# Wide matmuls in the up-projection: a high weight block times high and low activations at once, the halves summed on VectorE

## The reference

```
h = rmsnorm(x, ffn_norm_g[l])
up = causal_dwconv(h @ w_ffn_up[l], ffn_dw_w[l], ffn_dw_b[l])
gt, val = jnp.split(up, 2, axis=-1)
x = x + (jax.nn.silu(gt) * val) @ w_ffn_down[l]
```

## Time and profile before

| | |
|---|---|
| median of 3 runs | 926.17 us (925.93 to 927.03) |
| profiled execution | 928.54 us, its span 926.7 us |
| busy share of the span | PE 93%, DVE 68%, ACT 52%, POOL 44% |
| mean granted clock | 0.973 |
| instructions | 18327, of them 6732 matmuls |
| matmuls of `uh`, `ul` with the unit weights | 3 x 832, mean 283 to 285 ns |

### The profile page before, as it was taken

How to read it: one execution, slowest core, us unless ns; L and a number is a source line. 1 busy time by engine, 2 the same in 40 slices (tenths; PEclk the granted TensorE clock), 3 DMA queues, 4 the chain that set the end, 5 groups by cost and what they waited for, 6 DMA issues and landing times.

```text
span 926.7 us, 18327 instructions
## 1 busy us (share of the span) xinstructions
PE 864.2 (93%) x6732; PEld 827.4 (89%) x6732; DVE 628.1 (68%) x1198; ACT 486.0 (52%) x730; POOL 405.8 (44%) x94
## 2 busy tenths in 40 slices
PE   2799999799999999999979999997999999999996
PEld 1799988678999999999979998785999999999995
DVE  6586899925367876656537878994445687666564
ACT  4353357636456555645555333873635655455454
POOL 4477735445721131131257874543565031321323
PEclk8799999989999999999989999997999999999998
DMA  7355424313535555555425542432434546555551
GB/s 259 112 181 183 163 92 137 137 47 136 181 137 182 182 181 181 181 184 180 179 95 182 183 182 92 138 137 66 162 116 158 182 143 217 182 184 181 181 181 46
DMA packets 20512, 144.20 MB, mean 156 GB/s; under 512 B 2400, under 2 KB 2656, under 8 KB 3296
## 3 DMA queue, kind: packets, MB, share of 16 engines
q1 hardware_dynamic: 19872, 142.62, 43.3%
q10 hardware_dynamic: 576, 0.75, 0.2%
HBM read 142.31 MB, written 1.05 MB: 155 GB/s over the span
## 4 chain that ended last, share of the span: by engine, by line
PE 67%; DVE 16%; issue 10%; ACT 5%; DMA 1%; DVEq 0%; ACTq 0%
PE pu L720 18%; PE pu L721 17%; PE pu L722 17%; DVE pc L493 5%; ACT whi L225 2%; PE ps L720 2%; PE ps L722 2%; PE ps L721 2%; DVE wlo L622 1%; DVE ol L557 1%; DVE top L534 1%; PE pc L722 1%; PE pt L721 1%; PE pt L720 1%; PE pt L722 1%
## 5 line engine op out<-in xcount | busy, mean ns | idle before, releaser
L197 POOL TENSOR_TENSOR wlo<-raw,whi 128x2048 fp32r<-128x2048 f32 x88 | 405.1, 4606 | 512.6 <-ACT whi L225 512.6
L225 ACT ACTIVATE whi<-raw 128x2048 fp32r<-128x2048 f32 x134 | 254.7, 1902 | 29.1 <-PE pu L722 26.2
L720 PE MATMUL pu<-hh,whi 128*128 128x256 f32 x800 | 233.1, 291 | 24.4 <-ACT hh L242 22.6
L720 PE MATMUL pu<-uh,whi 128*128 128x256 f32 x832 | 237.2, 285 | 5.4 <-DVE ul L600 3.2
L721 PE MATMUL pu<-ul,whi 128*128 128x256 f32 x832 | 235.4, 283 | 0.0
L722 PE MATMUL pu<-uh,wlo 128*128 128x256 f32 x832 | 235.4, 283 | 0.0
L721 PE MATMUL pu<-hl,whi 128*128 128x256 f32 x800 | 228.1, 285 | 0.0
L722 PE MATMUL pu<-hh,wlo 128*128 128x256 f32 x800 | 228.0, 285 | 0.0
L493 DVE SCALAR_TENSOR_TENSOR pc<-upad,par,pc 128x256 f32<-128x256 f32 x464 | 186.9, 482 | 0.3
L720 PEld LDWEIGHTS pu<-hh,whi 128*128 128x128 f32 x800 | 155.1, 194 | 28.4 <-ACT hh L242 23.3
L720 PEld LDWEIGHTS pu<-uh,whi 128*128 128x128 f32 x832 | 159.6, 192 | 7.8 <-issue 7.5
(11 more groups left out here) (142 smaller groups left out, 1170.5 us busy)
## 6 DMA issues: line engine op xcount, KB each, us to landing
raw<-in_weights SPq DMA_DIRECT2D x134, 1024.0 KB, 4.8
x<-in_x_t SPq DMA_DIRECT2D x2, 512.0 KB, 5.6
out_y<-qk SPq DMA_DIRECT2D x2, 512.0 KB, 2.6
par_all<-in_params ACTq DMA_DIRECT2D x1, 472.0 KB, 10.3
const<-in_const ACTq DMA_DIRECT2D x1, 130.0 KB, 7.1
probs<-in_positions ACTq DMA_DIRECT2D x1, 128.0 KB, 4.8
gf<-in_final_g ACTq DMA_DIRECT2D x1, 4.0 KB, 12.4
```

The lines of the kernel that those rows point to most:

```text
L197: nc.gpsimd.tensor_tensor(wlo[s][:, :], raw[s][:, :], whi[s][:, :].bitcast(f32), ALU.subtract).then_inc(lo_ready[s], 1)
L225: A(whi[s][:, :], raw[s][:, :], ACT.Copy).then_inc(hi_ready[s], 1)
L720: MM(out, whi[s][:, w], hi, start=start, stop=False, skip_group_check=accumulate)
```

## The change

The normalised activations of the up-projection are kept side by side in one tile `uparts` (for each input block 256 high, then 256 low columns). For an up unit each high weight block is multiplied by both at once, in one matmul of 512 columns that fills a PSUM bank: columns 0 to 255 collect the high sums, 256 to 511 the sums of high weight x low activation. The low weight block x high activation stays a matmul of 256 columns that adds to the first half. A unit so has 32 matmuls in place of 48 and needs two banks, one for the gate, one for the value half. The two pairs of banks take the place of `pu[0..2]` and `po`: the second pair's last bank is `po`, so the layer's second up unit now waits for the norm factor (`rstd_ready`) too.

Since VectorE is to sum two halves of one bank, ScalarE first copies the low halves into SBUF (`take_low`, into `low_sums`, which lies in `gate`), VectorE adds them to the high halves in place in PSUM, and then scales as before. Banks in other parts of the program keep their use under new names. The diff, cut:

```diff
+                def take_low(k, ab, s, done_value):
+
+                    act.wait_ge(unit_done[s], done_value)
+                    A(low_sums[:, ab, :, :], pairs[ab][:, :, 1, :], ACT.Copy).then_inc(low_taken, 1)
+
...
+                    take_low(k, 0, 2, l * USES + j + 12)
                     hidden_tile(k, 0, col, col + FT * 4, k - 1, lambda: split_high(l, 2, j + 11))
                     act.wait_ge(unit_done[1], l * USES + j + 12)
                     hidden_high(k, 0, parity)
+                    take_low(k + 1, 1, 0, l * USES + j + 13)
                     hidden_tile(k + 1, 1, col + 4, col + FT * 4 + 4, k, None if last else lambda: split_high(l, 0, j + 12))
...
-                def scale_up(s, ab, done_value):
-
-                    dve.wait_ge(unit_done[s], done_value)
-                    V.tensor_tensor(up[:, ab, :, :], pu[s][:, :, :], rstd[:, :].unsqueeze(1).to_broadcast([P, 2, T]),
+                def scale_up(k, ab):
+
+                    dve.wait_ge(low_taken, k + 1)
+                    sums = pairs[ab][:, :, 0, :]
+                    V.tensor_tensor(sums, sums, low_sums[:, ab, :, :], ALU.add).then_inc(up_whole, 1)
+                    dve.wait_ge(up_whole, k + 1)
+                    V.tensor_tensor(up[:, ab, :, :], sums, rstd[:, :].unsqueeze(1).to_broadcast([P, 2, T]),
                                     ALU.mult).then_inc(up_ready, 1)
...
+                            w = slice((2 * k + m) * P, (2 * k + m) * P + P)
+                            MM(pair[:, m, :, :], whi[s][:, w], uparts[:, k, :, :], start=(k == 0), stop=False)
+                            last = MM(pair[:, m, 0, :], wlo[s][:, w], uh[:, k, :], start=False, stop=(k == NT - 1))
+                    last.then_inc(unit_done[s], 1)
...
                 pe.wait_ge(down_zero, l + 1)
-                standard(U_FFN + 1, uh, ul)
+                pe.wait_ge(x_ready, l * 8 + 4)
+                pe.wait_ge(rstd_ready, l * 3 + 3)
+                up_unit((U_FFN + 1) % RING, uses(l, U_FFN + 1), pairs[1])
```

More of the change, by code:

```diff
@@ L81, in hybrid_encoder @@
         oh, ol = sb("oh", [P, NT, T], f32r), sb("ol", [P, NT, T], f32r)
[L82 removed]
+        uparts = sb("uparts", [P, NT, 2, T], f32r)
+        uh, ul = uparts[:, :, 0, :], uparts[:, :, 1, :]
         fh, fl = oh[:, 0:4, :], ol[:, 0:4, :]
@@ L113, in hybrid_encoder @@
         up = gate[:, 0, 0:4, :].rearrange("p (a n) t -> p a n t", a=2)
+        low_sums = gate[:, 0, 4:8, :].rearrange("p (a n) t -> p a n t", a=2)
         pos_i, turns = probs[0][:, 0:2, :].bitcast(i32), probsT[0][:, 2:4, :]
         ang, aabs = sb("ang", [P, 2, P])[:, :, :], sb("aabs", [P, 2, P])[:, :, :]
-        pu = [pb(f"pu{s}") for s in range(RING)]
+        pairs = [ctx.enter_context(nc.psum_tensor(f"pair{i}", [P, 2, 2, T], f32)) for i in range(2)]
+        pu = [pairs[0][:, 0, :, :], pairs[0][:, 1, :, :], pairs[1][:, 0, :, :]]
+        po = pairs[1][:, 1, :, :]
         ps = [pb(f"ps{i}") for i in range(2)]
-        pt, po, pc = pb("pt"), pb("po"), pb("pc")
+        pt, pc = pb("pt"), pb("pc")
         down = [ps[0], ps[1], pt, pc]
@@ L141, in hybrid_encoder @@
         gate_ready, m_step = sem("gate_ready"), sem("m_step")
-        down_zero, down_done, up_ready, f_conv0, f_tap, f_silu, f_ready, fh_ready, fl_ready = [
-            sem(n) for n in ("down_zero", "down_done", "up_ready", "f_conv0", "f_tap", "f_silu", "f_ready", "fh_ready", "fl_ready")]
+        down_zero, down_done, low_taken, up_whole, up_ready, f_conv0, f_tap, f_silu, f_ready, fh_ready, fl_ready = [
+            sem(n) for n in ("down_zero", "down_done", "low_taken", "up_whole", "up_ready", "f_conv0", "f_tap", "f_silu", "f_ready", "fh_ready", "fl_ready")]
         y_ready, y_out_s = sem("y_ready"), sem("y_out")
@@ L462, in _ @@
                 V.tensor_scalar(par[:, PA_CW:PA_CW + NT * CONV_WIDTH], par[:, PA_CW:PA_CW + NT * CONV_WIDTH], 0.5, None, ALU.mult).then_inc(par_ready, 1)
-                for pairs in (top, less_top):
+                for both in (top, less_top):
                     for g in range(N_KV):
                         sinks = par[:, PA_SINK + GROUP_PAIRS * g:PA_SINK + GROUP_PAIRS * (g + 1)]
-                        V.tensor_copy(pairs[:, N_CHUNKS * g:N_CHUNKS * (g + 1), :, 1],
+                        V.tensor_copy(both[:, N_CHUNKS * g:N_CHUNKS * (g + 1), :, 1],
                                       sinks.unsqueeze(1).to_broadcast([P, N_CHUNKS, GROUP_PAIRS])).then_inc(par_ready, 1)
@@ L866, in _, with up_unit @@
                 scaled = parts_ready(uh_ready, l * 8 + 4, ul_ready, l * 8 + 4)
-                standard(U_FFN, uh, ul, scaled, lambda: sum_pair(po[:, 0, :], sq, 3, sq_ready, l * 12 + 12))
+                def up_unit(s, uses_before, pair, ready=None, between=None):
+                    pe.wait_ge(hi_ready[s], uses_before + 1)
+                    pe.wait_ge(lo_ready[s], uses_before + 1)
+                    for m in range(2):
+                        if m == 1 and between is not None:
+                            between()
+                        for k in range(NT):
+                            if ready is not None and m == 0 and k % 2 == 0:
+                                ready(k // 2)
+                            w = slice((2 * k + m) * P, (2 * k + m) * P + P)
+                            MM(pair[:, m, :, :], whi[s][:, w], uparts[:, k, :, :], start=(k == 0), stop=False)
+                            last = MM(pair[:, m, 0, :], wlo[s][:, w], uh[:, k, :], start=False, stop=(k == NT - 1))
+                    last.then_inc(unit_done[s], 1)
+                pe.wait_ge(x_ready, l * 8 + 3)
+                up_unit(U_FFN % RING, uses(l, U_FFN), pairs[0], scaled, lambda: sum_pair(po[:, 0, :], sq, 3, sq_ready, l * 12 + 12))
                 pe.wait_ge(down_zero, l + 1)
-                standard(U_FFN + 1, uh, ul)
+                pe.wait_ge(x_ready, l * 8 + 4)
+                pe.wait_ge(rstd_ready, l * 3 + 3)
+                up_unit((U_FFN + 1) % RING, uses(l, U_FFN + 1), pairs[1])
                 def down_unit(s, k, parity):
@@ L885, in ffn_step @@
                     pe.wait_ge(up_ready, k - 1)
-                    unit(2, n + 10, uh, ul)
+                    up_unit(2, n + 10, pairs[0])
                     pe.wait_ge(up_ready, k)
-                    unit(0, n + 11, uh, ul)
+                    up_unit(0, n + 11, pairs[1])
                     pe.wait_ge(hi_ready[1], n + 12)
```

11 lines of the change are left out of this document (6 added, 5 removed).

## The result

| | before | after |
|---|---|---|
| median, us | 926.60 (4 runs, 925.93 to 928.43) | 942.67 (4 runs, 942.57 to 943.28) |
| ratio | | 1.0164, 95% interval 1.0151 to 1.0177 |
| profiled execution, span, us | 928.54, 926.7 | 942.65, 940.7 |
| granted clock, mean | 0.973 | 0.966 |
| first up unit to final down unit, layer 1 | 187.48 | 192.66 |

The change makes the kernel 16.1 us slower. The direction was forecast, the size was not: 935.4 was predicted, with 930.5 to 940.0 as its range.

A forecast was written before the change was run, and what follows sets the result against it. The side chain through GpSimd, VectorE and ScalarE was to bound the FFN: 10.9 us added against 7.7 us of slack per layer, +6.6 us in two layers, clock +2.6; 926.17 + 6.6 + 2.6 = 935.4, range 930.5 to 940.0.

The forecast's parts named there:

- side chain: FFN: GpSimd low weights, VectorE and ScalarE work until GpSimd restarts; turn 16.04 us growing to 16.77, above TensorE's 16.45.
- The layer boundary: Between the layers: no term in the sum, which counted only the two FFNs and the clock.
- The add: VectorE in each up unit: the second tile's add is not hidden, +0.73 us a turn.
- The trio: TensorE in up units: one 512 and one 256 column matmul, 0.334 us instead of 0.360, saving 18.3 us in all.
- The floor of 0.112 us: TensorE: a minimum near 0.112 us per matmul with its own weight load, disappearing behind a long stream.
- the head: Start of each FFN: copy and add +1.2 us, second tile +0.7, so the first GpSimd start comes 1.9 us later.
- the first turn: FFN, first to second GpSimd start: scaling 1.8 us later behind copy and add, tile 3 adds 0.7, together +2.5.
- the eight further turns: FFN, second to tenth GpSimd start: copies and first add hidden, second add +0.73 us each, 5.8 in all.
- Two signs named ahead: FFN: VectorE's scaling no longer waits for TensorE; TensorE waits some 4 us before the final down unit.
- The clock: Final down unit: half clock after TensorE's wait costs 1.3 us per layer, +2.6 in all, bounds 0 and 1.7 each.
- TensorE sets the pace: Rival, FFN: chain turn under 16.45 us, most of the 18.3 us saving stays, near 914 us; chance 0.10.
- The wide matmul brings nothing: Rival, up units: trio stays 0.360 us, added waits on top, 939.2 us or 941.8 with the clock's fall; chance 0.07.

The follow-up runs named there:

- chain only: The changed kernel with each wide matmul written as two matmuls of 256 columns, copy and add kept: 942.49 us, ratio 1.0167 to before.
- final wait filled: The changed kernel with eight matmuls of 512 columns into a free bank before TensorE waits for a layer's last activations: 938.79 us, ratio 1.0116 to before.
- load held: The changed kernel with the second weight load behind layer 1's boundary held until ScalarE's first operation of layer 2: 941.13 us, ratio 1.014 to before.
- first kernel with fillers: The kernel before with filling matmuls: 12 at the start, 4 ahead of and 24 behind each layer's last statistics sums: 931.73 us, ratio 1.0038.

## Why the prediction was right in direction and wrong in size

**The reading of the bound was right.** A side chain through GpSimd, VectorE and ScalarE, with 7.7 us of slack per layer, was said to decide, and TensorE's saving to turn into waits. The run without the chain and the run without the wide matmul show it: -1.9 and +6.9 us per layer.

**Which steps failed.** Three terms of the sum were mis-sized. The layer boundary was put at nothing, and 2.85 us came there. The add was given 0.73 us a turn, and took 0.83 to 0.87. The trio was put at 0.334 us, and took 0.353. Without the first the time would have been 939.8 (an estimate, 942.67 less 2.85), just inside the range: the terms of the chain had used up the room in it, and the boundary took the time out.

**The worst guess: the trio.** The prediction took 0.213 us for the wide matmul plus 1 to 13 ns, since the 13 ns that 256 columns take beyond their stream "are something else" and would disappear under a long stream. The floor of 0.112 us doesn't bind these matmuls: in bfloat16 those of 256 columns follow after 0.109. The wide matmul took 0.237, above the upper bound, because at full clock the 4-byte format costs some 10% per column at either width (0.120 and 0.237, in bfloat16 0.109 and 0.215). The rows held a hint that was read the wrong way: at half clock the same 256 columns took 0.21 us, exactly their stream. TensorE's step became 17.07 and not 16.45, and so longer than the chain's turn, not shorter.

**What that did to the sum is small.** The FFN came out 5.17 us longer instead of 3.3. By GpSimd's rows of after and before: the head 0.24 longer than forecast (2.14 for 1.9), the first turn 0.15, the eight further turns 135.31 us instead of 134.16, the last piece 15.34 instead of 15.06: 1.8 in all. Of the 1.15 us in the eight turns some 0.4 is TensorE holding the last ones at 17.07, the rest is a turn of 16.87 instead of 16.77: the add costs 0.83 to 0.87 us per turn and not the 0.73 between its start and that of the scaling. The last 0.1 can be placed but not explained. Counted from GpSimd's start, the scaling of the odd tile comes at 9.92 us instead of 9.17 and ScalarE's SiLU at 13.60 instead of 12.84, both some 0.75 later. VectorE's product behind the SiLU comes at 14.10 instead of 13.27, because its wait for the SiLU is 0.40 us instead of 0.33. So the wrong trio, though the worst term, cost the sum only about 0.4 us per layer (an estimate: with turns of 16.86 throughout, the tenth GpSimd start would be at 313.49 + 8 x 16.86 = 448.4 instead of 448.80), because the chain hides TensorE's gain. Where it did mislead is the faster side: TensorE's saving, called 18.3 us, is some 4. Two signs named ahead came out otherwise for the same reason: VectorE's add still waits 1.2 to 1.9 us for TensorE's sums by way of the copy, and TensorE stands 2.47 us before the final down unit and not near 4, since its second up unit of the last step starts 1.3 us behind GpSimd and not beside it.

**The clock** fell at the final down unit in both layers, as predicted, and cost 1.45 us each instead of 1.3. A fall at the head was said to cost nothing, and it did. The reason given, a wait as long as that of rows 8, isn't enough: of the eight waits of 2.83 to 2.85 us at the head of the FFN in after, chain only, final wait filled and load held, two were followed by a fall and six were not, and the two of 1.94 and 1.95 us in the run without the copy both were. So that the two falls came where they were forecast was in part luck. What tells the cases apart is open.

**Not foreseen: the layer boundary.** 2.85 us of the 4.30 between the layers were no term of the sum. The prediction took it that everything behind the final down unit moves along unchanged. But the half clock stretches that unit by 1.4 us and not the loads beside it, and so ScalarE's jump to its loop's start came under a weight load. That is 1.6 us, measured from the final unit to the first matmul of layer 2 (18.48 us against 15.40, less the 1.4 of the clock); with the fall filled away or the load held it is gone. The other 1.2 us lie behind that matmul. There the half clock grew from 6.8 to 10.24 us, but they are within the 2 us of scatter of that part, and no run shows them to be the change's.

Together: 9.2 were predicted; + 3.7 in the FFNs, + 0.3 for the clock, + 2.9 from the boundary on (1.6 of it accounted for) are the 16.1 us found.

**The rivals.** "TensorE sets the pace" (914) is refuted twice over: even without any chain the wide form brings 2 us. "The wide matmul brings nothing" (939.2 or 941.8) was given 0.07 and came nearest to the time: the wide matmul saves 7 ns a trio and not 26. In part that is luck, for it has nothing at the boundary either, and the run that is its own case, the chain only, kept the full clock and was 6.9 us longer per layer, not 6.5. Still the case deserved more, since the trace of before had no matmul of this width and type at all, and its price was inferred from rows of another type.

## What to carry to other kernels

A change that trades time on the busiest engine for a longer chain beside it is to be judged by the chain's turn, measured start to start on the engine that restarts it, and by its slack over the whole loop, not by the busy share. An unseen instruction form is priced from rows of its own data type at the clock that it will run at, and where there is none the case "it brings nothing" is a likely one. Where a loop jumps back, look whether a large load is in flight: here 1.4 us more of work ahead of the jump put it under one.

## What the runs showed of the hardware that was not expected

- At 2.4 GHz TensorE streams the 4-byte split format slower than bfloat16: 0.120 against 0.109 us for 256 columns, 0.237 against 0.215 for 512, each with its own weight load. At 1.2 GHz the 4-byte format took 0.21 for 256.
- An engine's jump to a loop start can wait for a weight load: ScalarE stood 3.72 us (after) and 3.83 (first kernel with fillers) with a 1 MB load in flight, 1.23 and 1.27 with that load held back.
- Matmuls that feed nothing kept the granted clock full. Before the final down unit they cost nothing (it starts 192.61 us behind the first up unit, without them 192.66), behind the last layer's statistics 0.7 us. In the three waits at the end of attention they raised the mean clock from 0.989 to 0.997 and gave 4.6 us.
- What a fall of the clock costs depends on what lies under it: 1.44 us over the final down unit, nothing at the head of the FFN, where a wait follows (192.66 us with it, 192.65 without).
- A wait of 2.83 us was followed by half clock in one layer of after and by full clock in the other; 2.35 us kept it, 2.47 and 1.94 lost it. The runs don't say what decides.
